# Modulation row stored from ScalarE's queue, its products in four state steps; 19 expert slots filled ahead of the expert stage

## The reference

```python
def modulation(cvec, p):
    return jnp.split(jax.nn.silu(cvec) @ p['mod_w'] + p['mod_b'], 6, axis=-1)

# layer, in the latent path
mixed, _ = token_mixer_2(h, p, ctx_states)
x = x + m_lat[2] * rmsnorm(mixed, p['norm1_post'])
h2 = rmsnorm(x, p['norm2_pre']) * (1.0 + m_lat[4]) + m_lat[3]
x = x + m_lat[5] * rmsnorm(expert_choice_moe(h2, p), p['norm2_post'])

def expert_choice_moe(h, p):
    affinity = jax.nn.softmax((h @ p['router_w']).astype(jnp.float32), axis=-1)
    gates, idx = lax.top_k(jnp.swapaxes(affinity, 1, 2), cap)        # 16 experts, cap = 32 tokens
    xe = jax.vmap(lambda hb, ib: hb[ib])(h, idx)
    hid = jax.nn.silu(xe @ exp_w1) * (xe @ exp_w3)                   # 1024 -> 2048, per expert
    ye = (hid @ exp_w2) * gates[..., None]                           # 2048 -> 1024
    ... # added to the chosen tokens
```

## Time and profile before

| | us |
|---|---|
| runs | 2295.44, 2297.39, 2299.78 |
| median | 2297.39 |
| the profiled execution, its own time | 2301.36 |
| its span (first to last instruction) | 2299.5 |
| PE busy | 1755.1 (76%) |
| DVE busy | 829.5 (36%) |
| ACT busy | 643.6 (28%) |
| DMA over the span | 588.39 MB, mean 256 GB/s |
| start of the expert stage | 1378.06 |

### The profile page before, as it was taken

The page is one execution under the profiler, slowest core; times in us unless marked ns, Lnnn a source line. Parts: engine busy times, 40 slices in busy tenths (PEclk is TensorE's granted clock), DMA queues, the critical chain, the costliest instruction groups (busy, mean ns, idle before and its releaser), DMA issues. The chain is left out here.

```text
span 2299.5 us, 36430 instructions
## 1 busy us (share of the span) xinstructions
PE 1755.1 (76%) x15933; PEld 1177.9 (51%) x15933; DVE 829.5 (36%) x1198; ACT 643.6 (28%) x1043; POOL 232.0 (10%) x222
## 2 busy tenths in 40 slices
PE   6998997978999977797879966655556665565565
PEld 6997995867879855796769741111111111111111
DVE  4654435775655665676655540000000000000001
ACT  4333444564424354334443320000000000000001
POOL 0100004430121032102430000000000000000000
PEclk9999998999999988797979969778877777878877
DMA  6654651235855522243025369999999999999997
GB/s 200 199 190 136 202 176 55 88 129 181 274 166 195 173 88 76 95 132 116 6 73 161 137 280 422 427 428 428 428 428 428 428 428 427 428 427 428 428 428 296
DMA packets 181746, 588.39 MB, mean 256 GB/s; under 512 B 11339, under 2 KB 144134, under 8 KB 156886
## 3 DMA queue, kind: packets, MB, share of 16 engines
q1 hardware_dynamic: 180074, 585.12, 66.1%
q10 hardware_dynamic: 1516, 0.96, 0.2%
HBM read 584.88 MB, written 1.17 MB: 255 GB/s over the span
## 5 line engine op out<-in xcount | busy, mean ns | idle before, releaser
L193 DVE TENSOR_TENSOR split_lo<-ring,split_hi 128x2048 fp32r<-128x2048 f32 x126 | 293.5, 2332 | 199.1 <-ACT split_hi L186 198.1
L3516 PE MATMUL ps<-ex_ring,ex_xe 128*32 128x512 f32 x1440 | 229.5, 770 | 156.1 <-DMA ex_ring<-in_exp_w 156.1
L3597 DVE TENSOR_TENSOR ex_hid<-ps,ex_silu 128x512 f32<-128x512 f32 x16 | 11.1, 692 | 866.5 <-PE ps L3516 866.5
L232 PE MATMUL ps<-xt_hi,split_hi 128*128 128x256 f32 x984 | 283.6, 288 | 11.7 <-DVE xt_lo L395 7.3
L186 ACT CAST split_hi<-ring 128x2048 fp32r<-128x2048 f32 x127 | 240.2, 1896 | 175.8 <-PE ps L234 120.6
L233 PE MATMUL ps<-xt_lo,split_hi 128*128 128x256 f32 x984 | 279.3, 284 | 0.0
L234 PE MATMUL ps<-xt_hi,split_lo 128*128 128x256 f32 x984 | 278.9, 283 | 0.0
L3516 PEld LDWEIGHTS ps<-ex_ring,ex_xe 128*32 128x32 f32 x1440 | 44.3, 126 | 337.5 <-DMA ex_ring<-in_exp_w 245.6
L232 PEld LDWEIGHTS ps<-xt_hi,split_hi 128*128 128x128 f32 x984 | 188.3, 191 | 22.4 <-issue 20.6
L232 PE MATMUL ps<-split_hi,xt_hi 128*128 128x256 f32 (+1 forms) x560 | 176.5, 315 | 17.2 <-DVE split_lo L193 6.5
L233 PEld LDWEIGHTS ps<-xt_lo,split_hi 128*128 128x128 f32 x984 | 188.5, 192 | 1.2 <-issue 1.2
(11 more groups left out here) (746 smaller groups left out, 2759.6 us busy)
## 6 DMA issues: line engine op xcount, KB each, us to landing
ex_ring<-in_exp_w SPq DMA_DIRECT2D x133, 2048.0 KB, 46.0
ring<-in_exp_w SPq DMA_DIRECT2D x39, 2048.0 KB, 45.9
ring<-in_w_in SPq DMA_DIRECT2D x55, 1024.0 KB, 5.3
ex_late<-in_exp_w SPq DMA_DIRECT2D x19, 2048.0 KB, 46.2
ring<-in_ffn_w_gate SPq DMA_DIRECT2D x22, 1024.0 KB, 5.7
ring<-in_ffn_w_up SPq DMA_DIRECT2D x22, 1024.0 KB, 5.3
ring<-in_ffn_w_down SPq DMA_DIRECT2D x22, 1024.0 KB, 5.0
ring<-in_mod_w SPq DMA_DIRECT2D x16, 1024.0 KB, 5.6
```

Source lines behind the costliest of these rows:

```text
L193: eng.tensor_tensor(g.wlo[:, s % H, 0:n], g.ring[:, i % R, 0:n], g.whi[:, s % H, 0:n].bitcast(F32), ALU.subtract).then_inc(g.tiles_split, 1)
L232: nc.tensor.matmul(out, lhs[0], rhs[0], start=start, stop=False, skip_group_check=shared)
L3516: mm = mm_(ps[32 * q:32 * q + 32, 4 + u, :], xe[:, k], w[:, 512 * q:512 * q + 512], start=k == 0, stop=k == KC - 1)
L3597: v.tensor_tensor(hid[:], ps[:, 5, :], silu[:], ALU.mult).then_inc(S["hid"], 1)
```

## The change

In the class and in the four inputs blocks:

- The store of `mod_row` and its wait move from SP to ACT, as the last entry of ACT's list of the block; ACT's copy into `mod_row` moves ahead of the copies of the token matrices (ahead of `j` = 1). The block behind no longer has a wait for the store; instead ACT waits for the store before it copies the next row or writes the split buffers again, and SP before it reads the rows back.
- In the backward passes the eight products steps stand behind the first four state steps, two each.

In the expert weights:

- `ex_ring` gets a fixed place that is free from the merge stage on. There SP loads two of its pairs: slots 8 and 9 behind the first tile of `hy_proj` and a wait for the variance (`S["var"]`, DVE), and slots 6 and 7 behind the last tile of `w_out` and waits for `yh` and `yturn`.
- The router's `xn` and `xt` lie in the place of `xet`, which is written later, and `ex_late` has a fixed place whose upper half is free in the router stage. There SP first loads slot 19 alone (1 MB), then the remaining five pairs; slot 18 is loaded at the start of the expert stage (1 MB in place of the pair's 2 MB).

```diff
@@ LateModulation
     def act_copy(self, act):
         act.wait_ge(self.g.direct_used, 4 * self.n + 4)
+        if self.n:
+            act.wait_ge(self.g.mod_stored, 16 * self.n)
         self.nc.scalar.copy(self.g.mod_row[:], self.out).then_inc(self.g.mod_copied, 1)
-    def store(self, sp):
-        sp.wait_ge(self.g.mod_copied, self.n + 1)
-        sp.dma_start(late_sums(self.g)[self.n].rearrange("(a n) -> a n", n=T), self.g.mod_row[0:97:32, :]).then_inc(self.g.mod_stored, 16)
-
-    def wait_stored(self, sp):
-        sp.wait_ge(self.g.mod_stored, 16 * self.n + 16)
+    def store(self, act):
+        act.wait_ge(self.g.mod_copied, self.n + 1)
+        act.dma_start(late_sums(self.g)[self.n].rearrange("(a n) -> a n", n=T), self.g.mod_row[0:97:32, :]).then_inc(self.g.mod_stored, 16)
@@ recurrence_inputs
             late.load_next(sp)
-            late.store(sp)
...
                 for n in range(NCH):
                     before.pe_step(pe, n)
-                    late.pe_step(pe, n)
+                    for k in range(2 * n, min(2 * n + 2, KC)):
+                        late.pe_step(pe, k)
...
             for j in range(d, 4):
+                if j == 1:
+                    late.act_copy(act)
                 for t in range(TT):
                     act.wait_ge(S["tokturn"], q + 1)
...
-            late.act_copy(act)
+            late.store(act)
@@ recurrence_chunks
-        @block.sync
-        def _(sp):
-            late.wait_stored(sp)
@@ recurrence_states, ACT
+            act.wait_ge(g.mod_stored, 32)
@@ merge_phase, SP
+            sp.wait_ge(g.mod_stored, 64)
...
+            load_tiles(g, sp, hy0 + 1)
+            sp.wait_ge(S["var"], 1)
+            load_expert_pair(nc, g, sp, I, R + 4)
             load_tiles(g, sp, out0 + 4)
+            sp.wait_ge(S["yh"], 1)
+            sp.wait_ge(S["yturn"], 1)
+            load_expert_pair(nc, g, sp, I, R + 2)
@@ merge_phase, ACT
+            act.wait_ge(g.mod_stored, 64)
             for k in range(10):
@@ router_phase
-        with ExitStack() as early:
-            xt = early.enter_context(nc.sbuf_tensor("rt_xt", [P, KC, T], F32))
+        xt = xet[:, 4:8].rearrange("p k n -> p (k n)").rearrange("p (k n) -> p k n", k=KC)
...
+            load_first_late(nc, g, sp, I, 1)
             for n in range(R, EX_LATE, 2):
-                load_expert_pair(nc, g, sp, I, n)
+                if n not in (R + 2, R + 4):
+                    load_expert_pair(nc, g, sp, I, n)
@@ expert_phase
-        g.ex_late = sb("late", [P, ER - EX_LATE, WT])
...
+                if n == EX_LATE:
+                    load_first_late(nc, g, sp, I, 0)
+                    continue
                 load_expert_pair(nc, g, sp, I, n)
@@ new
+def load_first_late(nc, g, sp, I, half):
+
+    rows = I["exp_w2_2"][0].rearrange("e (k p h) n -> p (e k) (h n)", h=4, p=P)[:, EX_LATE % KC // 2, :]
+    sp.dma_start(expert_slots(g, EX_LATE + half, 1), rows[:, WT * half:WT * half + WT]).then_inc(g.ex_loaded[EX_LATE], 16)
```

More of the change, by code:

```diff
@@ L1601, in allocate @@
     g.issued = 0
+    g.ex_base = 32 * (-(-nc.sbuf_base // 32))
     split_buffers(nc, g)
@@ L1674 @@
 EX_LATE = 18
+EX_LATE_BASE = 229344 - 2 * 4 * WT
 CTX0 = 4
@@ L2585, in recurrence_chunks @@
         eye = g.pat[:, 0:CH]
-        late = LateModulation(nc, g, LATE_STAGE[name], 0)
         RAW, SPREAD, FLIPPED, TWO, LOW3, FACTOR, FTIL, KM = 1, 2, 4, 6, 7, 8, 9, 10
@@ L3358, in _ @@
             sp.dma_start(iota[:], I["k_iota"]).then_inc(S["consts"], 16)
+            assert nc.sbuf_base <= EX_LATE_BASE + 4 * WT
+            load_first_late(nc, g, sp, I, 1)
             for n in range(R, EX_LATE, 2):
-                load_expert_pair(nc, g, sp, I, n)
+                if n not in (R + 2, R + 4):
+                    load_expert_pair(nc, g, sp, I, n)
         @block.tensor
@@ L3469, in expert_phase @@
         ss, post = sb("ss", [P, 8]), sb("post", [P, D])
-        g.ex_late = sb("late", [P, ER - EX_LATE, WT])
+        assert nc.sbuf_base <= EX_LATE_BASE
         tmp = g.ring[:, 0, :].rearrange("p (t n) -> p t n", t=TT)
@@ L3478, in loaded @@
             if n % 2 == 0:
-                eng.wait_ge(g.ex_loaded[n % ER], 16 * (n // ER + 1))
+                eng.wait_ge(g.ex_loaded[n % ER], 16 * (n // ER + 1) + (16 if n % ER == EX_LATE else 0))
             elif n == NE * TPE - 1:
@@ L3667, in second_block @@
             recurrence_phase(nc, g, I, z, store, part, st, False, "rl")
+            g.ex_ring = nc.alloc_sbuf_tensor_at("ex_ring", [P, EX_LATE - R, WT], F32, offset=g.ex_base)
             merge_phase(nc, g, I, z, yh, store, part, st)
@@ L3671, in second_block @@
             dump("d")
-        g.ex_ring = sb("ex_ring", [P, EX_LATE - R, WT])
+        room = sb("ex_ring_room", [P, EX_LATE - R, WT])
+        assert room.manual_sbuf_range is None and nc.sbuf_base >= g.ex_base + 4 * WT * (EX_LATE - R)
         g.ex_used = ctx.enter_context(nc.semaphore("ex_used"))
@@ L3675, in second_block @@
         g.iota = sb("iota", [P, CAP])
-        with ExitStack() as c1:
-            g.xn = c1.enter_context(nc.sbuf_tensor("xn_moe", [P, TT, D], F32))
-            router_phase(nc, g, I, xet, mt, aff)
+        g.xn = xet[:, 0:4].rearrange("p k n -> p (k n)").rearrange("p (t n) -> p t n", t=TT)
+        g.ex_late = nc.alloc_sbuf_tensor_at("ex_late", [P, ER - EX_LATE, WT], F32, offset=EX_LATE_BASE)
+        router_phase(nc, g, I, xet, mt, aff)
         expert_phase(nc, g, I, xet, mt, aff, out_dram)
```

## The result

| | before | changed |
|---|---|---|
| median, us | 2297.39 (5 runs) | 2286.42 (5 runs) |
| lowest to highest | 2295.44 to 2301.98 | 2282.54 to 2289.20 |
| profiled execution, its own time | 2301.36 | 2289.20 |
| its span | 2299.5 | 2287.4 |
| start of the expert stage | 1378.1 | 1369.4 |

The ratio is 0.9950, with an interval of 0.9938 to 0.9961: 11.0 us faster. The forecast was 2286.7. Every ratio here is against the kernel before, measured beside it on the same chip; the experiments ran on three chips, on which the kernel before took 2297.58, 2296.74 and 2296.61 us, so ratios compare better than medians. A sum can be right while its terms are not, so the execution is cut at the barriers between the blocks.

The account below looks back on a forecast made before the run. The end was taken as the expert stage's start plus remaining bytes at 428 GB/s plus a tail. Slots 2.45 + block ends 5.5 + earlier loads 2.7 = 10.7 us, so 2297.4 - 10.7 = 2286.7 us; range 2282 to 2293.

Parts of the forecast that it names:

- The slots: Expert stage: 19 slots instead of 18 full at its start, one slot's transfer saved, 2.45 us (bounds 0 and 2.45).
- Moved pairs: Two expert pairs moved from router to merge stage only make loads that were already early earlier; worth 0.
- The pair ahead of the second hy_proj tile: Merge stage: the pair delays that tile by 4.9 us, within ACT's slack, so it costs nothing.
- Block ends: Inputs blocks: moved store and products end them earlier: rl1i 2.2, rc1i 2.7, rc0i and rl0i 0.3 each; together 5.5 us.
- The store at 0.54: Inputs blocks: the store, last on ACT's empty queue, was taken to cost 0.54 us.
- Doubled groups in rc1i at 1.0: rc1i: two product groups behind each of the first four state steps make ACT end 1.0 us later.
- rl1i's doubled groups: rl1i: eight groups instead of six ahead of the seventh state move make it, and DVE's end, 1.1 us later.
- The earlier loads: Block behind rl1i: w_in loads end earlier, so PE's 4.22 us stall shrinks to 1.49; 2.7 us (bounds 0 and 4.2).
- ACT pays what SP paid: rc1i and rl1i: busy DMA engines make ACT's store take 2.8 and 2.5 us; total gain 6.7 us, 2290.7; chance 0.08.
- The stall stays: Block behind rl1i: the 4.22 us gap has another cause or still meets the loads; gain 8.0 us, 2289.4; chance 0.17.
- the stall moves into the state steps: Backward inputs blocks: early loads delay the state steps' code, 4.2 us in one or both; 2290.9 to 2295.1; chance 0.12.
- All five slots count: Router loads did hold up the expert stage's start, so the moved pairs pay 9.8 us too; 2276.9; chance 0.03.

Follow-up runs that it names:

- e5: Changed kernel with slot 19 left empty, both halves of that pair issued at the start of the expert stage; 2288.8 us, ratio 0.9964.
- e6: Changed kernel with the two moved expert pairs loaded in the router stage again; 2284.22 us, ratio 0.9950.
- e2: Changed kernel with only the store given back to SP, behind the four loads; 2287.58 us, ratio 0.9952.
- f1: The changed kernel, unaltered, measured and profiled once more; 2282.98 us, ratio 0.9940.
- e4: Changed kernel with products behind eight state steps again and the backward passes' w_in loads issued late in the following block; 2292.0 us, ratio 0.9974.
- e1: Changed kernel with products behind eight state steps and ACT's row copy last again in the backward blocks, store still on ACT; 2290.2 us, ratio 0.9966.
- e3: Changed kernel with the four w_in loads of the two backward passes issued at the start of the following block; 2295.12 us, ratio 0.9990.
- e9: On top of e8, all twenty expert slots full at the expert stage's start and the first refill split into two 1 MB loads; 2282.62 us, ratio 0.9936.
- e8: Changed kernel with forward-pass products ahead of the first transposes and rc1's w_in loads moved to the states block behind the chunks; 2284.23 us, ratio 0.9941.
- f2: The e9 kernel, unaltered, measured and profiled once more; 2281.13 us, ratio 0.9927.

## Why the prediction was right

The total was off by 0.3 us, and that is partly luck: errors in both directions met, and the second measurement of the same kernels gave 13.6 us in place of 11.0.

**The slots.** Forecast 2.45, measured 2.4 to 2.5 (e5 against the middle of the others). The other 1.5 us of the expert stage are PE's lower clock in the tail of before's one profile; whether they are part of the change is not shown. Moved pairs: forecast 0, and e6 shows 0. The idle time of the DMA ahead of the expert stage grew to 10.5 us rather than 13 (the loads end at about 1359, the stage starts at 1369.4). The pair ahead of the second hy_proj tile did not show: merge is 0.7 us shorter, and 131.9 to 133.5 in the other kernels.

**Block ends.** Forecast 5.5, and too low. Measured from block to block, rc1i gave 3.4 to 4.4 us over all kernels of the table (forecast 2.7), rl1i 1.9 to 3.3 wherever the clock rose early (2.2), rc0i 1.1 to 1.7 (0.3) and rl0i 0.5 to 1.4 (0.3). Three terms of the step were mis-sized:

- *The store at 0.54.* I set it behind ACT's last copy. The sequencer issues it beside that copy, so it ends with the copy or a little before it.
- *What follows the last engine.* I let each block begin 0.9 us after its last engine, as SP's 1155.60 was followed by 1156.49. That holds for a DMA issue, on ACT as on SP: PE starts 0.87 to 0.98 us after the end of the store's issue wherever it comes last (1.21 us once, in rc0i of before). After DVE's or ACT's own last work it starts 0.36 to 0.38 us later (rl1i here, the other three blocks in e2). Store and start together were priced at 1.4 us behind ACT's last copy and are 0.74 in rc1i, 0.99 in rc0i and 0.89 in rl0i; without a store on ACT they are 0.36.
- *Doubled groups in rc1i at 1.0.* ACT ended 20.76 us into the block before (897.16 - 876.40) and ends 21.04 us into it now: 0.3.

The term of the step that held is the one of rl1i's doubled groups. DVE ended 26.97 us into the block before; in f1 it ends at 28.01, 1.04 later, where 1.1 was forecast. e4, with eight steps and the same ACT store, starts the next block after 28.24 us, and the four-step kernels but for the first profile after 27.86 to 29.26. For the end of rl1i the four steps bring nothing; in rc1i, with the store on ACT, they bring 0.1 to 0.6 us (21.76 to 22.20 against 22.32 and 22.40). They pay mostly through the earlier loads. The lower bound of this step, a loss of 2.7, had the long store in the two backward blocks only; with 2.81 us in the forward blocks as well it would be some 6.4.

**The earlier loads.** Forecast 2.7; rl1c is 2.97 shorter in the first profile and 2.2 in f1. In rc1c, where I took nothing, the gap fell from 3.15 to 2.46 and the block is 0.8 shorter. The inference from one coincidence was right, as e1 and e3 show. PE's first issue gap in the block (in e3 the first two), by how far the loads reach into the block (they take some 13.6 us from their first issue):

| loads reach into the block | rc1c, gap | rl1c, gap |
|---|---|---|
| not at all, or not yet | 1.70, 1.96, 2.21, 2.48 (e4, e9, e8, f2) | 1.11 (e4) |
| 0.3 us (changed) | | 1.44 |
| 2.4 us (changed) | 2.46 | |
| 3.7 and 4.6 us (before) | 3.15 | 4.22 |
| 7.1 and 7.4 us (e1) | 4.71 | 4.14 |
| 13 us and more (e3) | 5.25 and 2.37 | 2.70 and 5.15 |

That these gaps are instructions arriving late can be checked in the record, which has the packets of an instruction queue. The page of before:

```profile
q8 instruction: 126, 2.06, 0.4%
```

These are 126 packets of 16 KB, one for every 253 of PE's 31,866 matmuls and weight loads; the other engines have under 2,500 instructions together in the page's count. The twelve profiles have 132 issue gaps of PE over 0.6 us. Of these, 120 end 1.2 to 1.6 us after such a packet has landed; the other 12 are one gap a profile near 350 us, far from the change. In rl1c the two gaps stand behind PE's 335th and 591st instruction of the block, 256 apart, in every kernel. Packets by queue in before's rl1c, first from 1156.0 to 1160.6, then from 1160.6 to 1161.9 (packets, MB, share of 16 engines):

```profile
q1 hardware_dynamic: 1582, 1.60, 110.3%
```

```profile
q1 hardware_dynamic: 173, 0.16, 39.2%
q8 instruction: 1, 0.02, 5.4%
```

While the loads (q1) run, no instruction packet comes. It starts at 1160.68, 4.2 us after the block's start, as the loads run out, lands at 1161.81, and PE goes on at 1163.30. In the changed kernel the packet of the same place starts 1.7 us after the block's start, lands at 1155.26, and PE goes on at 1156.68. In e3, where the second gap is the long one, from 1158.9 to 1163.1 and from there to 1164.4:

```profile
q1 hardware_dynamic: 1444, 1.46, 110.0%
```

```profile
q1 hardware_dynamic: 442, 0.44, 103.8%
q8 instruction: 1, 0.02, 5.6%
```

This packet starts 4.2 us after PE has gone on (1158.97 to 1163.15); in the changed kernel it is 1.15 us (1156.68 to 1157.83). The packets themselves take 0.9 to 1.5 us in these blocks with loads or without; what the loads put off is their start. In e4 no instruction packet starts from 914.7 to 922.9, while the loads pass; the next starts at 923.00, and PE's new gap ends at 925.47. In the changed kernel the loads pass from 1141.2 to 1152.9 with one such packet among them, and no gap follows. So the stall is PE waiting for instructions whose transfer is kept back by the w_in loads, as the prediction read it. It does not stand at the block's branch but 335 instructions behind it.

The Trainium skill ("Runtime: NRT & Kernel Launch", Instruction fetch mechanics) calls the crossing of an instruction block mostly hidden. Over the whole program the trace of before agrees: 10 of its 126 packets end a gap over 0.6 us. At the start of the chunk blocks it does not: with idle DMA engines 1.0 to 2.5 us stay visible, and with busy ones up to 5.3, so by these runs the rule does not hold beside a full stream of loads.

**What I missed.** I used this mechanism for one block and not for its neighbours. rc0i ends 1.1 us earlier while its loads do not, so they reach 2.3 us into rc0c instead of 1.1. The gap there went from 1.46 to 2.72 us and rc0c is 1.0 us longer: a gain at a barrier is partly given back behind it. The same holds for rl0c with 1.49 and 1.73. Together this offset about half of the underestimate at the block ends (by f1's lengths 8.3 us gained for 5.5 forecast). The rest of the difference lies in stretches that differ between executions whatever the change, by 3 to 5.5 us each: the blocks ahead of rc0i (815.3 to 820.8), project (101.4 to 101.8 with the granted clock at half for 3 or 4 us of it, 103.6 to 104.3 with 8 or 9) and router (38.4, 40.5 or 42 with 22, 28 or 33 us at half).

**The rivals.** "ACT pays what SP paid" is refuted by e1's 0.50 us under full DMA. The Trainium skill ("DMA: Bandwidth & Descriptors", Issuing engines are not separate DMA queues) says that another engine saves only sequencer time, usually small; it saved 2.0 to 2.3 us of SP's, which mattered because the sequencer was what the barrier waited for; e2 shows that the same was to be had on SP, with the loads issued earlier. "The stall stays" and "the stall moves into the state steps": neither is seen. The changed kernel has no issue gap of 0.8 us or more there. "All five slots count" falls with e6.

## What to carry to other kernels

At a barrier look for the queue that arrives last, and for what its last instruction stands behind: a 4 KB store took 2.5 to 2.8 us to issue directly behind four large loads on one queue and 0.5 on another, and as the last entry of the queue that arrives last it still cost 0.4 to 0.6 us. Look for the stretch of code that bears the bulk loads: in the wrong one they put off PE's own instructions and cost 2 to 5 us with nothing waiting for the data, and wherever a block is made shorter the loads that were issued in it reach further into the next. Of buffers filled ahead of a streaming stage, count only those full when it starts, each worth its transfer, less the time for which the stream then has nothing to issue.

## What the runs showed of the hardware

- A DMA issue on SP took 2.54 to 2.81 us directly behind four loads of 1 MB, even when issued 7 us ahead of need (2.69 in rl1i, 2.74 in rc1i, e2), and 0.54 where the loads had been issued 5 to 6 us before (rc0i and rl0i before the change); on ACT's queue it took 0.49 to 0.51 in the backward blocks at the same load of the DMA engines.
- ACT's queue can issue a DMA while ACT's copy ahead of it still runs (issued from 1150.88 to 1151.39, beside a copy from 1150.91 to 1151.50).
- Behind a barrier PE started 0.36 to 0.38 us after the last work of DVE or ACT, and 0.87 to 0.98 us (once 1.21) after the end of the last DMA issue, on SP or ACT, where that came last.
- PE's instructions come in packets of 16 KB, one for some 256 instructions. In rc1c and rl1c the first packet started 1.2 to 2.2 us after the block's start where the loads had ended by then, and 3.0 to 5.3 us after it where they ran on (before, e1, e3); PE went on 1.2 to 1.6 us after it had landed.
- One code at one place, PE busy throughout, had the granted clock of TensorE rise to 1.00 some 3.4 us into a block in one execution and 9.6 us into it in another: 2.3 us or more of a 28 us block. Stage lengths of one profile are good to about that. The eight products at the end took 3.79 us at a granted clock of 0.62 to 0.69 and 1.99 at 0.80 to 1.00.
